# Seven block products for twelve projection chunks, ahead of the attention

## The reference

```python
h = rms_norm(x, g_pre_mix)                        # x: 1024 rows x 1024, float32
proj = h @ w_in                                   # 1024 x 3072
hc, bg, cg, q, k, v = split(proj, 6)              # 512 columns each
y_conv = bg * conv3(cg * hc, w_conv)              # depthwise, causal, 3 taps
y_attn = band_attention(q, k, v, rel_bias)        # 8 heads of 64; chunk of 64 sees itself and 8 to the left
y = concat(group_norm(y_conv), group_norm(y_attn)) @ w_out
x = x + rms_norm(y, g_post_mix)
h = rms_norm(x, g_pre_ffn)
f = (silu(h @ w_gate) * (h @ w_up)) @ w_ffn_out   # 2816 wide
out = x + rms_norm(f, g_post_ffn)
```

## Time and profile before

| | |
|---|---|
| time, median of 3 runs | 1122.86 us (1122.79 to 1123.09) |
| span of the profiled execution | 1120.9 us; around it 2.0 us to the median of the runs |
| TensorE busy | 1112.3 us (99%), 5725 matmuls and transposes |
| VectorE busy | 699.1 us (62%) |
| ScalarE busy | 459.8 us (41%) |
| GpSimd busy | 162.9 us (15%) |
| chain that ended last | TensorE 98% |
| moved by DMA | 153.63 MB, mean 137 GB/s |

### The profile page before, as it was taken

The page is one execution under the profiler, slowest core; times in us unless marked ns, Lnnn a source line. Parts: engine busy times, 40 slices in busy tenths (PEclk is TensorE's granted clock), DMA queues, the critical chain, the costliest instruction groups (busy, mean ns, idle before and its releaser), DMA issues.

```text
span 1120.9 us, 16059 instructions
## 1 busy us (share of the span) xinstructions
PE 1112.3 (99%) x5725; PEld 922.8 (82%) x5725; DVE 699.1 (62%) x1167; ACT 459.8 (41%) x870; POOL 162.9 (15%) x259
## 2 busy tenths in 40 slices
PE   9999999999999999999999999999999999999997
PEld 7887887887888888888888888888888888888886
DVE  6314445435345667786878787777777777555584
ACT  5332452543545555663322323222323257444441
POOL 3400011101110112311122112211211120000031
PEclk9999999999999999999999999999999999999999
DMA  7220101110110255342564446444634699777632
GB/s 263 95 76 20 39 20 39 38 39 20 39 38 20 65 198 188 132 131 90 165 215 159 139 132 215 142 127 162 201 117 147 214 315 373 235 228 231 217 116 84
DMA packets 112087, 153.63 MB, mean 137 GB/s; under 512 B 6984, under 2 KB 72536, under 8 KB 112032
## 3 DMA queue, kind: packets, MB, share of 16 engines
q1 hardware_dynamic: 95440, 95.96, 26.8%
q0 software_dynamic: 15424, 52.74, 14.1%
q10 hardware_dynamic: 1168, 4.20, 1.0%
HBM read 112.74 MB, written 40.13 MB: 136 GB/s over the span
## 4 chain that ended last, share of the span: by engine, by line
PE 98%; DMA 1%; DVE 0%; ACT 0%; issue 0%; SPq 0%; POOL 0%; DVEq 0%; POOLq 0%
PE psum L1171 34%; PE psum L801 24%; PE psum L1198 18%; PE psum L1056 8%; PE psum L976 4%; PE psum L844 3%; PE psum L815 2%; PE psum L825 2%; PE psum L790 1%; PE psum L952 1%; DMA arena<-in_x 1%; PE psum L852 0%; PE psum L945 0%; PE psum L958 0%; PE psum L834 0%; DVE arena L2241 0%
## 5 line engine op out<-in xcount | busy, mean ns | idle before, releaser
L801 PE MATMUL psum<-hT,ws 128*128 128x512 f32 (+1 forms) x1104 | 253.9, 385 | 0.0
L801 PEld LDWEIGHTS psum<-hT,ws 128*128 128x128 f32 x1104 | 197.3, 188 | 39.0 <-issue 0.7
L1171 PE MATMUL psum<-arena_r,ws 128*128 128x512 f32 x960 | 224.1, 389 | 0.0
L1171 PEld LDWEIGHTS psum<-arena_r,ws 128*128 128x128 f32 x960 | 180.2, 188 | 37.4
L1171 PE MATMUL psum<-hT,ws 128*128 128x512 f32 x720 | 169.9, 389 | 0.0
L1171 PEld LDWEIGHTS psum<-hT,ws 128*128 128x128 f32 x720 | 135.1, 188 | 28.0
L1198 PE MATMUL psum<-hT 128*128 128x512 f32 (+1 forms) x600 | 135.2, 385 | 0.0
L1198 PEld LDWEIGHTS psum<-hT 128*128 128x128 f32 x600 | 111.3, 188 | 22.5
L2050 DVE TENSOR_TENSOR misc<-misc,psum 128x512 f32<-128x512 f32 x100 | 68.6, 686 | 48.7 <-PE psum L1171 46.1
L1544 ACT ACTIVATE ws<-o_raw 128x512 fp32r<-128x512 f32 x40 | 25.2, 630 | 138.5 <-DVE o_raw L2028 138.0
L1056 PE MATMUL psum<-ws,hT 128*128 128x512 f32 x348 | 81.7, 392 | 0.0
(11 more groups left out here) (222 smaller groups left out, 1361.5 us busy)
## 6 DMA issues: line engine op xcount, KB each, us to landing
raw<-in_w_ffn_in SPq DMA_DIRECT2D x44, 512.0 KB, 4.0
act_scratch<-arena POOLq DMA_DIRECT2D x77, 256.0 KB, 3.2
raw<-in_w_in SPq DMA_DIRECT2D x22, 512.0 KB, 3.8
arena<-in_w_ffn_out POOLq DMA_DIRECT2D x22, 512.0 KB, 5.5
arena<-act_scratch SPq DMA_DIRECT2D x38, 256.0 KB, 3.5
arena<-in_x SPq DMA_DIRECT2D x16, 512.0 KB, 6.3
raw<-in_w_out SPq DMA_DIRECT2D x16, 512.0 KB, 3.6
raw<-act_scratch SPq DMA_DIRECT2D x26, 256.0 KB, 3.6
```

Source lines behind the costliest of these rows:

```text
L801: last = mm(PP[pair][:, at:end] if to is None else to, w[wp], hT[:, hp, k, at:end], start=(k == 0 and (wp, hp) == (0, 0)), stop=(k == KT - ...
L1171: last = mm(blocks(bank), w[:, k * P:(k + 1) * P], b_operand(i, part, k), start=fresh_bank and k == 0 and w is hi and part == 0, stop=k == ...
```

## The change

Six rounds of seven block products now stand between the values and the attention, and compute twelve of the twenty chunks: hc and cg of the convolution's groups 0 to 2 (rounds 0 to 2), bg 0 and 1 (round 3), bg 2 and hc 3 (round 4), q and k of head pair 0 (round 5). For that, the sums of the row tiles (now also `x_first_t`, `x_second_t`, `x_low_t`, `x_high_t`) are made while the values are computed. The convolution of groups 0 to 2 is gated, tapped and normed in the rounds. Rows of the arena are scarce there, so the values and the three convolution results are stored in DRAM and loaded back at the end of round 5. The other eight chunks (q and k of pairs 1 to 3, cg and bg of group 3) stay in the attention as pieces, two a step and less in places. The bias table is stored 128 times over, so that a DMA can read the shifted rows in their final order, after round 5; no engine turns rows round. The attention's result of a block is normed in the next one and transposed in the one after.

Constants and the fill of the attention:

```diff
-    FIRST = 2
-    OUT0 = FIRST + 5 * (PAIRS - 1) + 3
+    OUT0 = 2 * PAIRS
...
+    FRONT = 6
+    RAW0 = FRONT + FIN0 // 2 + PLAIN
+    FRONT_ORDER = [(0, 6, 3, 1, 2, 4, 5)] + [tuple(range(OPS))] * (FRONT - 1)
...
+    v_d = nc.dram_tensor("value_scratch", [NT * P, 512], F32, kind="Internal").ap()
+    y_d = nc.dram_tensor("conv_scratch", [(PAIRS - 1) * P, SEQ], F32, kind="Internal").ap()
     ERW = BAND + P - 1
-    ext_d = nc.dram_tensor("bias_scratch", [HEADS, ERW], F32, kind="Internal").ap()
+    ext_d = nc.dram_tensor("bias_scratch", [HEADS, P, ERW], F32, kind="Internal").ap()
...
-    FILLS = [[(4,)] * 7 + [(2, 2), (4, 2, 2)]] * 2 + [[(4,)] * 7 + [(2, 2), (2, 1, 1)], [(4,)] + [(2,)] * NT]
+    AHEAD = 3
+    FILLS = [[(1,)] + [(2,)] * 7 + [(1, 0, 0)]] * LAST + [[(1,)] + [(2,)] * 4 + [(1,)] * 4]
```

The bias on GpSimd:

```diff
-    ext = row(CR, ERW)[0:HEADS, :]
+    ext = row(7, ERW, 256)[0:HEADS, :]
...
+            far = BAND - CLIP
+            chain(nc.gpsimd.tensor_copy(ext[:, 0:far], relb[:, REL - 1:REL].broadcast_to([HEADS, far])
+                                  ))
+            chain(nc.gpsimd.tensor_copy(ext[:, far:ERW], relb[:, REL - 2:CLIP - P:-1]))
+            pool.dma_start(ext_d, ext.rearrange("h (o x) -> h o x", o=1).broadcast_to([HEADS, P, ERW])
+                           ).then_inc(ext_stored, 16)
...
+            for i in range(5, NT):
+                x_factor(i)
             pool.wait_ge(ext_stored, 16)
...
+            pool.wait_ge(prod, multiplied(FRONT - 1, 4))
+            heads = ((0, 2), (2, HEADS))
...
+            for n, (first, end) in enumerate(heads):
+                pool.dma_start(b3[:, first:end, :], bass.AP(ext_d.tensor, first * P * ERW + P - 1,
+                                                            [[ERW - 1, P], [P * ERW, end - first], [1, BAND]])
+                               ).then_inc(bias_landed[n], 16)
```

The sums of the rows on ScalarE, and its order in the first stage:

```diff
+            def x_copy_even(m):
...
+                if m > 1:
+                    act.wait_ge(t_lo, 2 * m - 2)
+                go(XE[m], PP[2 * m % 3], ACT.Copy).then_inc(e_copied, 1)
+
+            def x_high_t(m):
+
+                act.wait_ge(t_made, m + 1)
+                if m == 1:
+                    act.wait_ge(ext_stored, 16)
+                if m == 2:
+                    act.wait_ge(v_stored[0], 32)
+                go(t34[0][:, :, m, :], XE[m].rearrange("p (k s) -> p k s", s=P), ACT.Copy).then_inc(t_hi, 1)
+                go(t12[:, m // 2, 0, :, m % 2 * P:(m % 2 + 1) * P], XO[m].rearrange("p (k s) -> p k s", s=P),
+                   ACT.Copy).then_inc(t_hi, 1)
...
-            sq_x(2), sq_x(3), high_hT(2), copy_v(0), sq_x(4), copy_v(1)
+            x_copy_even(0)
+            sq_x(2), sq_x(3), high_hT(2), x_copy_even(1), copy_v(0), sq_x(4), copy_v(1)
+            x_high_t(0)
             for i in range(3, NT):
                 high_hT(i)
+                if i in (4, 6):
+                    x_copy_even(i // 2)
                 if i + 2 < NT:
                     sq_x(i + 2)
                 copy_v(i - 1)
+                if i in (4, 6):
+                    x_high_t(i // 2 - 1)
+            x_high_t(3)
```

The order on VectorE (`x_first_t` and `x_second_t` are two subtractions of 512 columns each, `x_low_t` two of 1024):

```diff
-            norm_x(2), norm_x(3), low_hT(2), norm_x(4)
+            norm_x(2), norm_x(3), x_first_t(0), x_second_t(0), low_hT(2), norm_x(4), x_low_t(0)
             for i in range(3, NT):
                 low_hT(i)
+                if i % 2:
+                    x_first_t(i // 2)
                 if i + 2 < NT:
                     norm_x(i + 2)
+                if i % 2:
+                    x_second_t(i // 2)
+                elif i >= 4:
+                    x_low_t(i // 2 - 1)
...
+            front_s(0)
+            x_low_t(3)
+            for i in FRONT_ORDER[0]:
+                front_low(0, i)
...
+            def gated_round(n):
+
+                make_u2(n)
+                front_low(n + 1, 0)
+                if n > 0:
+                    tap(n - 1, 0)
+                make_u3(n)
...
+                front_s(n + 1)
+                front_low(n + 1, 1), front_low(n + 1, 2)
+                if n > 0:
+                    tap(n - 1, 1)
+                make_c22(n)
+                front_low(n + 1, 3), front_low(n + 1, 4)
+                if n > 0:
+                    tap(n - 1, 2)
+                make_c21(n)
+                front_low(n + 1, 5)
+                dve.wait_ge(c11_done, n + 1)
+                chain(gated(0, s11, u3))
+                make_c12(n)
+                gated(1, u2, c22).then_inc(front_out, 1)
```

The rounds on TensorE, with what waits for the convolution, and ScalarE's order in rounds 4 and 5:

```diff
+            def front_multiply(n, i):
+
+                pe.wait_ge(front_lo, split(n, i))
...
+                if n > 0 and i in (0, 1, 2, 4):
+                    pe.wait_ge({0: c11_done, 1: u2_made, 2: c21_made, 4: c12_made}[i], n)
+                if i == 3:
+                    pe.wait_ge(p1_copied, n + 1)
+                if i == 5:
+                    pe.wait_ge(u3_made, n + 1)
+                if n > 0 and i == 6:
+                    pe.wait_ge(c22_made, n + 1)
...
+            behind = {(4, 1): (stats, 0), (4, 3): (stats, 1), (4, 4): (norms, 0),
+                      (5, 0): (norms, 1), (5, 1): (stats, 2), (5, 4): (norms, 2)}
...
+            front_copy_first(4), square_y(0)
+            front_high(5, 0), front_high(5, 1), square_y(1), front_high(5, 2), front_high(5, 3)
+            spread_conv(0), front_high(5, 4), spread_conv(1), front_high(5, 6)
+            front_copy_first(5), square_y(2), front_high(5, 5)
```

The way back from DRAM, on SP:

```diff
+            sp.wait_ge(v_stored[0], 32)
+            sp.wait_ge(v_stored[1], 48)
+            sp.wait_ge(prod, multiplied(FRONT - 1, 5))
+            load_v(0), load_v(1), load_v(2)
+            load_conv(0)
+            load_v(3)
+            load_conv(1), load_conv(2)
```

More of the change, by code:

```diff
@@ L369, in trunk_layer @@
         o_rs = sem("o_rs")
-        y_rs = sem("y_rs")
         x2_rs = sem("x2_rs")
@@ L794, in project @@
                         passes=((0, 0), (0, 1), (1, 0))):
-                parts = first_w[-1 - slot] if slot < 0 else [ws[:, slot, part, :] for part in range(2)]
+                parts = [ws[:, slot, part, :] for part in range(2)]
                 w = [part[:, k * P:(k + 1) * P] for part in parts]
@@ L1028, in _ @@
                 last.then_inc(v_psum, 1)
-            pe.wait_ge(hT_done, NT)
-            for g in range(FIRST):
-                pe.wait_ge(w_split, g + 1)
-                for k in range(KT):
-                    project(-1 - g, k, g + 1)
-            for q in range(8):
+            pe.wait_ge(v_copied, NT - 2)
+            for j in range(4):
+                for part in (HIGH, LOW_W, LOW_H):
+                    last = values(NT - 1, (j,), part)
+                last.then_inc(v_used if j < 3 else v_psum, 1)
@@ new lines, in front_multiply @@
+            def front_multiply(n, i):
+                pe.wait_ge(front_lo, split(n, i))
+                if n == 0 and i == 0:
+                    bank_of_h(NT - 2)
+                if n == 0 and i == 6:
+                    bank_of_h(NT - 1)
+                if n == 0 and i == 1:
+                    pe.wait_ge(t_lo, NT)
+                if n > 0 and i in (0, 1, 2, 4):
[6 more added lines that the diff above has]
+                    pe.wait_ge(c22_made, n + 1)
+                hi, lo = front_w(n, i)
+                fresh_bank = i != 3 and (n == 0 or i != 6)
+                for k in range(4):
+                    for w, part in ((hi, 0), (hi, 1), (lo, 0)):
+                        last = mm(blocks(front_bank(n, i)), w[:, k * P:(k + 1) * P], b_operand(i, part, k),
+                                  start=fresh_bank and k == 0 and w is hi and part == 0,
+                                  stop=k == 3 and w is lo, skip_group_check=True)
+                last.then_inc(prod, 1)
@@ L1035, in _ @@
+            for n in range(FRONT):
+                for i in FRONT_ORDER[n]:
+                    front_multiply(n, i)
+                    if (n, i) in behind:
+                        task, t = behind[n, i]
+                        task(t)
+            for q in range(AHEAD):
                 piece(q)
@@ new lines, in make_c12, with gated, times, tap @@
+            def make_c12(n):
+                bank_sum(n, 6 if n else 4, u2, u2, BANK[3] if n else front_bank(0, 4), c12_made)
+            def gated(e, a, b):
+                return tt(tiles_of(row(CU), e), blocks(a), blocks(b), ALU.mult)
+            def times(t, e, block):
+                v = tiles_of(row(CONV_ROWS[t]), e)
+                return tt(v, v, blocks(block), ALU.mult)
+            def tap(t, n):
+                w, v, u = params[:, t, TAPS - 1 - n:TAPS - n], row(CONV_ROWS[t]), row(CU)
+                if n == 0:
+                    chain(ts(v, u, w, None, ALU.mult))
+                else:
+                    chain(stt(v[:, n:SEQ], u[:, 0:SEQ - n], w, v[:, n:SEQ], ALU.mult, ALU.add))
@@ new lines, in _ @@
+            times(0, 0, BANK[0]).then_inc(c11_done, 1)
+            make_c22(3)
+            front_low(4, 3), front_low(4, 4)
+            chain(times(1, 1, c22))
+            make_c21(3)
+            front_low(4, 5)
```

(10 more changed lines are left out.)

803 lines of the change are left out of this document (472 added, 331 removed).

## The result

The changed kernel takes 1176.14 us (median of 4 runs, 1175.73 to 1176.5), the kernel before in the same session 1122.82 us (1122.57 to 1123.09): ratio 1.0475, interval 1.046 to 1.049. It is slower by 53.3 us, where +41 was forecast. The profiled execution took 1175.89 us, its span is 1173.8 us.

What follows compares the result with a forecast made beforehand. TensorE's unbroken matmuls bound the kernel, so each new wait costs its full length. 47.5 + 1 + 2.2 + 2.1 + 5.0 - 16.3 = +41.5 gave a span of 1162.4, a time of 1164 us; range 1121 to 1178, own range 1147 to 1176.

Steps and rivals of the forecast that it cites:

- rival 3: GpSimd itself is held issuing 1024 rows, so TensorE stops before tile 5's transposes: about 1173 us; chance 0.06.
- The store decides, and ScalarE is what it holds: Bias table's store takes 56 us (bounds 41 and 63), lands at 87.3; ScalarE waits before `x_high_t(1)`, TensorE at tile 5: +47.5 us.
- Three ScalarE operations behind it, 3.2 us: After the store lands, ScalarE does `x_high_t(1)`, two copies and `high_hT(5)`; TensorE goes on 3.2 us after landing.
- Nothing for the tiles ahead of the stop: Values of the tiles before tile 5: the sum held no term for a TensorE wait there.
- The clock's restart, +1: TensorE restarts at the 1.2 GHz level after the long stop: +1 us, from nothing to 5.7, most hidden behind the next item.
- Values to the first product, +2.2: After the stop TensorE is done at L+20.7, VectorE at L+22.9 (L the landing): TensorE waits 2.2 us, bounds 0 and 4.
- Round 4, +2.1: Second statistics' square comes behind ScalarE's copy of operand 1; TensorE waits 2.1 us after the fourth product, bounds 0 and 4.
- Attention, +5.0: Half the filling matmuls: waits at three block ends, the first block's step 0, the last block's steps 5 to 8; bounds 0 and 9.
- -16.3 saved, the rounds at 0, the way back at 0: 504 matmuls instead of 576 save 16.3 us; rounds keep pace; values and bias come back in time, both at 0.
- Rivals 1: The store is hidden, spread over all engines: 10.3 us, landing 41.6, time 1118 (1112 to 1119), faster; chance 0.15.
- rival 2: The store uses eight engines at their normal rate: 18.8 us, landing 50.1, wait 10.3, time 1126 (1122 to 1131); chance 0.13.
- The engine rule: A transfer's number of engines is the largest up to 16 that divides both outer sizes, here 8 for the bias store.

Runs made afterwards that it cites:

- kernel with one copy: Against the changed kernel: each bias row stored once (24 KB), all partitions read the same unshifted row, shift left out; 1122.45 us in one run.
- the last kernel: Against the kernel with 128 partitions, square, first product's operands and attention fill moved: VectorE reads the first convolution statistics before round 5's front sum; 1112.71 us, ratio 0.9911.

## Why the prediction was right

The time (1176.14) lies in the range of 1121 to 1178, at its upper end, and just outside my narrower one of 1147 to 1176 (whose lower end should have been 1144 by its own terms, 1164 - 15 - 5). The number alone is nearer to rival 3's 1173 than to 1164; it is the trace that decides for the forecast. Step by step:

- **The store decides, and ScalarE is what it holds**: right. Its length was the term of the sum that was mis-sized: 56 us and 2.0 were taken, 62.8 and 2.0 came. Issue at 28.90 instead of 29.3, landing at 93.7 instead of 87.3. What was wrong is the choice between the bounds: 50 GB/s, the lower one, was the right one; "128 packets in a row have no ramp" was an argument with no row behind it. The packet spread of the 24 KB store with the last packet's own time, 50 GB/s, met the rate; with 0.5 us read from slices of 0.035 us that is partly luck. The other reading of the same store, 9.6 GB/s an engine from the share of busy time, was too high by half: an engine moved 6.5. The wait became 52.9, not 47.5.
- **Three ScalarE operations behind it, 3.2 us**: 3.06.
- **Nothing for the tiles ahead of the stop**: wrong by 0.7. TensorE waits 0.72 us at tile 2, now that the copies of even tiles stand ahead of other work on ScalarE.
- **The clock's restart, +1**: 2.15 in the values of tile 5, so 1.1 short, and nothing hid behind the next item. VectorE's line, which should have covered it, runs through the same values: ScalarE copies them at 104.79, only then rounds pair 2 (105.28), and VectorE goes on only then, at 106.37. I had that rounding done at L+11.5; it was done at L+13.5, with L = 93.81.
- **Values to the first product, +2.2**: 2.14. The wait is the difference of two lines that both came 2 us later than counted, for the reason just given: TensorE was done at L+22.7 instead of L+20.7, VectorE at L+24.8 instead of L+22.9. The operations behind the rounding took what I counted. It had no term for the clock after it, 1.7 us.
- **Round 4, +2.1**: 1.84, but only half explained. I counted ScalarE's line up to the square and missed VectorE's read of the bank, due at the same time. Both end within 0.1 us of each other, the square at 211.46 and the read at 211.39. And again no term for the clock, 1.6 us.
- **Attention, +5.0**: 4.0. The three turnings cost 2.1 (1.65 taken), steps 6 and 8 of the last block 1.6 (1.66 taken); the first bias and exp of a block cost 0.3 in all, not 1.6: the one piece covers them.
- **-16.3 saved, the rounds at 0, the way back at 0**: no wait inside the rounds but the one named, none for values or bias heads. But from the first product to the FFN it took 2.0 us more than saving, waits and clock explain. So of the 11.4 us that the sum is short of the span, the wait has 5.4. The other 6 are 0.7, 1.1, 1.7, 1.6 and 2.0 too little, less 1.3 too much in the attention and in round 4.

Rivals 1 and 2 are out by the landing at 93.7. Rival 3 is out as GpSimd issues in 1.20 us and turns to its next work at 30.11. The engine rule that I cited for rival 2, the Trainium skill's DMA: Bandwidth & Descriptors, section Why a DMA increments its semaphore by 16 and not by 1, fits the eight busy engines, but was not the limit: with 16 partitions, and twice the engines, an engine still moved only 6.6 GB/s, and with 32 partitions the same engines moved twice that. By the port rule that I cited from the Trainium skill (SBUF — State Buffer, Door 1: The DMA port swizzle) the transfer takes 58 us; the runs had 62.8, 8% more.

One thing stays open: half of the 2.0 us between the first product and the FFN, which are in no wait and in no low clock.

## What to carry to other kernels

Before a transfer that a wait hangs on is made larger, look at which partitions it reads, not at how busy the transfer engines are: eight rows sent 128 times are read from a sixteenth of the partitions, and having the rows on all of them first cost next to nothing here (with 128 partitions the store is issued at 29.07 instead of 28.90) and gave 54 us. A new wait of 2 us on the bounding engine is to be counted with what the lowered clock takes behind it, here nearly as much again in most of the profiled executions; and when a wait doesn't go as its releaser is moved, look for a second one due at the same moment.

## What the runs showed of the hardware

A store from 8, 16, 32, 64 and 128 partitions, the same 3.14 MB, ran at 50, 100, 194, 188 and 280 GB/s. From 128 it moved 356 GB/s (31 to 36 us) as long as nothing was stored beside it.

While the store from 8 partitions ran, a store of 256 KB by another queue took 26.6 us instead of 2.6 (kernel with one copy), and the slow store kept its 49 to 51 GB/s.

TensorE's clock was at its lower level not only in the long stop but for a part of the stretch behind waits of 1.8 to 2.1 us: means of 0.76 and 0.72 in the changed kernel, 0.74 and 0.83 with 128 partitions. In these four the same work took 1.6 to 1.7 us longer. At the second statistics of the kernels with 32 and 64 partitions and with one copy it was 3.3 us (statistics and 12 products 8.0 us, against 4.75 with the square moved). It didn't do so each time: behind a wait of 1.83 us the profiled runs of two kernels had 1.00. The times of single executions go with their mean clock over the whole run: with the square moved 1119.36 us at 0.999 and 1123.35 at 0.995, with 128 partitions 1120.8 to 1120.9 at 0.997 to 0.998 and the seven others, 1121.8 to 1122.7, at 0.995 to 0.996. In the last kernel, where the waits of this size are gone, all five have 0.998 or 0.999 and lie within 0.8 us. Narrow runs alone show nothing: the changed kernel's lie within 0.8 us too, with both waits.
